# Retention values centred ahead, short pair norms, an output projection begun on half its weight rest, smaller first transfers and a shorter final norm

## The reference, cut to what matters

```python
def retention(q, k, v, g):                      # 6 heads of 64
    ...                                         # rotary, decay-weighted scores sc, causal
    y = (y_intra + y_cross).reshape(b, s, RET_HEADS, HEAD_DIM)
    y = layer_norm(y).reshape(b, s, RET_WIDTH)  # over the 64 columns of a head
    return (jax.nn.silu(g) * y).astype(dt)

def hybrid_layer(x, ...):
    u = rms_norm(x, g_mix_pre) @ w_in
    ...
    mix = jnp.concatenate([y_att, y_conv, y_ret], axis=-1) @ w_out
    x = x + rms_norm(mix, g_mix_post)
    ...
```

## Time and profile before

| | us |
|---|---|
| time, median of 3 runs | 2420.83 |
| profiled execution, its time | 2420.81 |
| its span in the trace | 2419.0 |
| TensorE matmul busy | 2397.8 (99%) |
| VectorE busy | 1587.0 (66%) |
| ScalarE busy | 1084.9 (45%) |
| GpSimd busy | 339.9 (14%) |
| granted TensorE clock, mean | 0.999 of full speed |
| DMA, mean over the span | 108 GB/s |

### The profile page before, as it was taken

How to read it: one execution, slowest core, us unless ns; L and a number is a source line. 1 busy time by engine, 2 the same in 40 slices (tenths; PEclk the granted TensorE clock), 3 DMA queues, 4 the chain that set the end, 5 groups by cost and what they waited for, 6 DMA issues and landing times.

```text
span 2419.0 us, 34256 instructions
## 1 busy us (share of the span) xinstructions
PE 2397.8 (99%) x13622; PEld 2023.0 (84%) x13622; DVE 1587.0 (66%) x2239; ACT 1084.9 (45%) x1615; POOL 339.9 (14%) x259
## 2 busy tenths in 40 slices
PE   9999999999999999999999999999999999999998
PEld 7877988998886889889988888877778788889997
DVE  7764775665976477556643447769995476359685
ACT  4345553544445456345532235522335564325443
POOL 1231020001122102000111123400000121120001
PEclk9999999999999999999999999999999999999999
DMA  4311223323230222232222235643442153222322
GB/s 168 144 44 70 88 87 105 111 83 121 79 137 30 105 71 104 88 122 97 85 100 103 90 109 173 207 173 118 141 142 96 31 179 124 102 99 81 118 88 87
DMA packets 46738, 260.15 MB, mean 108 GB/s; under 512 B 5440, under 2 KB 8000, under 8 KB 22656
## 3 DMA queue, kind: packets, MB, share of 16 engines
q1 hardware_dynamic: 44192, 248.94, 29.3%
q0 software_dynamic: 640, 5.51, 0.6%
q10 hardware_dynamic: 1760, 3.67, 0.5%
HBM read 240.27 MB, written 16.78 MB: 106 GB/s over the span
## 4 chain that ended last, share of the span: by engine, by line
PE 89%; DVE 5%; ACT 2%; issue 2%; DMA 1%; POOL 0%; SPq 0%; DVEq 0%; ACTq 0%
PE gemm L486 58%; PE gemm L1094 5%; PE gemm L1095 5%; PE gemm L1096 5%; DVE w_lo L436 1%; PE gemm L770 1%; PE gemm L781 1%; PE gemm L772 1%; DVE out_sb L1904 1%; ACT w_hi L428 1%; PE turned L1389 1%; PE mixed L1403 1%; PE score L1380 1%; PE gemm L663 1%; PE gemm L664 1%
## 5 line engine op out<-in xcount | busy, mean ns | idle before, releaser
L436 DVE TENSOR_TENSOR w_lo<-w_raw,w_hi 128x2048 fp32r<-128x2048 f32 (+4 forms) x157 | 340.0, 2166 | 199.1 <-ACT w_hi L428 199.0
L486 PE MATMUL gemm<-h_hi,w_hi 128*128 128x512 f32 x1136 | 454.5, 400 | 1.9 <-DVE w_lo L436 1.4
L486 PE MATMUL gemm<-h_hi,w_lo 128*128 128x512 f32 x1136 | 443.3, 390 | 0.0
L486 PE MATMUL gemm<-h_lo,w_hi 128*128 128x512 f32 x1136 | 442.7, 390 | 0.0
L428 ACT ACTIVATE w_hi<-w_raw 128x2048 fp32r<-128x2048 f32 (+4 forms) x167 | 292.9, 1754 | 190.4 <-PE gemm L486 168.5
L486 PEld LDWEIGHTS gemm<-h_hi,w_hi 128*128 128x128 f32 x1136 | 213.7, 188 | 57.4 <-issue 9.1
L486 PEld LDWEIGHTS gemm<-h_hi,w_lo 128*128 128x128 f32 x1136 | 213.2, 188 | 45.8
L486 PEld LDWEIGHTS gemm<-h_lo,w_hi 128*128 128x128 f32 x1136 | 213.7, 188 | 41.8 <-issue 1.0
L486 PE MATMUL gemm<-f_hi,w_hi 128*128 128x512 f32 x480 | 187.2, 390 | 0.6
L486 PE MATMUL gemm<-f_hi,w_lo 128*128 128x512 f32 x480 | 186.8, 389 | 0.0
L486 PE MATMUL gemm<-f_lo,w_hi 128*128 128x512 f32 x480 | 186.8, 389 | 0.0
(11 more groups left out here) (544 smaller groups left out, 5295.9 us busy)
## 6 DMA issues: line engine op xcount, KB each, us to landing
w_raw<-in_w SPq DMA_DIRECT2D x179, 1024.0 KB, 4.8
w_raw<-in_w SPq DMA_DIRECT2D x18, 512.0 KB, 3.8
w_raw<-in_w SPq DMA_DIRECT2D x12, 768.0 KB, 4.2
trig_kept<-made SPq DMA_DIRECT2D x16, 512.0 KB, 5.9
trig<-trig_kept SPq DMA_DIRECT2D x16, 512.0 KB, 6.1
w_raw<-in_w SPq DMA_DIRECT2D x8, 640.0 KB, 4.6
bias_t<-in_att_bias SPq DMA_DIRECT2D x2, 1536.0 KB, 8.9
decay_t<-in_c_decay SPq DMA_DIRECT2D x2, 1536.0 KB, 8.8
```

The costliest lines, as they stand in the source:

```text
L436: dve.tensor_tensor(flat(w_lo, b), flat(w_raw, b), flat(w_hi, b).bitcast(F32), ALU.subtract).then_inc(S["w_rest"], 1)
L486: mm = pe.matmul(dst, lhs, rhs, start=b.first and k == 0 and j == 0, stop=b.last and k == b.kt - 1 and j == 2)
```

## The change

1. **Retention.** The values are centred before they are used: `centre_values` takes the mean over the 64 columns of each head from v, for a pair of heads in one reduction and one fused product on VectorE, at weight block 10 and after steps s = 5 and s = 9. `pair_mean` and `centre` go. ScalarE squares the pair straight from PSUM in `pair_out`. `pair_var` becomes one plain 128x512 matmul with `head_ones`, whose result is already spread, so `pair_spread` goes; Ln and Exp now take 128x512. GpSimd's gate product waits for the copy, no longer for the squares.
2. **Output projection.** `partial` on the first block waits for `half_rest` and, from tile 4 on, for `w_rest`. The second norm steps among the partials go; only `pair_var(3)` stays, after tiles 0 and 1.
3. **Opening.** Block 0 comes as a quarter, a quarter and a half, x tiles 0 and 1 separately; `ones` and `ident` come after all of x and both blocks. ScalarE does all roundings of x before the squares. `keep_clock` runs 4 matmuls, not 6, and the wait for `ones` moves to the sum, which moves two steps later.
4. **Memory sum.** It moves half a tile into the third block of `ffn1_down`.
5. **End.** ScalarE also multiplies x by the final gain (`x2_sq`), 6 tiles during the last blocks, the last two per half. `last_sums` goes: `final_total` takes three plain matmuls per half. `finished` takes one product per group of tiles (two groups of 4; then groups of 3, 3 and 2), with one store per group. The sum of half 0 now stands after the first of the two tiles of half 1, before it stood one step (3 matmuls) ahead of the end of the second.

The diff, cut to its core:

```diff
-            (1, 0), (1, 1), (0, 6), (0, 7), (1, 2), "sum", (1, 3), (1, 4), "turn", (1, 5), (1, 6), (1, 7)]
+            (1, 0), (1, 1), (0, 6), (0, 7), (1, 2), (1, 3), (1, 4), "sum", (1, 5), (1, 6), "turn", (1, 7)]
...
+        CUTS = [(0, WSIZE // 4), (WSIZE // 4, WSIZE // 2), (WSIZE // 2, WSIZE)]
+        FIRST_CUTS, SECOND_CUTS = CUTS, [(0, WSIZE // 2), (WSIZE // 2, WSIZE)]
...
-            load_part(sp, plan[0], False)
-            load_x(0)
-            load_part(sp, plan[0], True)
+            load_part(sp, plan[0], 0)
+            sp.dma_start(x_sb[:, 0, :], x_rows[:, 0, :]).then_inc(x_first_in, 16)
+            sp.dma_start(x_sb[:, 1, :], x_rows[:, 1, :]).then_inc(x_in[0], 16)
+            load_part(sp, plan[0], 1)
+            load_x(2)
+            load_part(sp, plan[0], 2)
+            load_x(4)
+            load_part(sp, plan[1], 0)
+            load_x(6)
+            load_part(sp, plan[1], 1)
             sp.dma_start(ones[:], A["c_ones"]).then_inc(consts_in, 16)
...
-            keep_clock(pe, t_ps[:], rs[:, 0:P], rs[:], 6)
-            pe.wait_ge(consts_in, 32)
+            keep_clock(pe, t_ps[:], rs[:, 0:P], rs[:], 4)
...
             def ret_mixed(s):
+                if j == 0 and h % 2 == 0:
+                    pe.wait_ge(S["v_centred"], cnt("v_centred", h // 2 + 1))
...
             def pair_var(j):
                 pe.wait_ge(S["ln_sq_s"], cnt("ln_sq_s", 2 + j))
-                for q in range(TOKT):
-                    mm = pe.matmul(t_ps[:, 2 * q:2 * q + 2], sq_tile(4 + j)[:, P * q:P * q + P],
-                                   head_ones[:, 0:P:HD], start=True, stop=True)
-                mm.then_inc(S["ln_var"], 1)
+                if j > 1:
+                    pe.wait_ge(S["ln_root"], cnt("ln_root", j))
+                pe.matmul(t_ps[:], head_ones[:], sq_tile(4 + j), start=True, stop=True).then_inc(S["ln_var"], 1)
...
-                if p == 2 and at_step == 0:
-                    pair_spread(1)
                 if p and at_step == TOKT // 2:
-                    pair_mean(p)
-                if p and at_step == TOKT + TOKT // 2:
                     pair_var(p)
...
-            partial(pe, first, h_hi, h_lo, (0, 1), ready=cnt("h_ready", KD))
-            pair_spread(2)
-            partial(pe, first, h_hi, h_lo, (2,), ready=cnt("h_ready", KD))
-            pair_mean(3)
-            partial(pe, first, h_hi, h_lo, (3, 4), ready=cnt("h_ready", KD))
+            partial(pe, first, h_hi, h_lo, (0, 1), ready=cnt("h_ready", KD), front=3 * lay + 1)
             pair_var(3)
-            partial(pe, first, h_hi, h_lo, (5,), ready=cnt("h_ready", KD))
-            partial(pe, second, h_hi, h_lo, (0, 1))
-            pair_spread(3)
-            partial(pe, second, h_hi, h_lo, (2,))
+            partial(pe, first, h_hi, h_lo, (2, 3, 4, 5), ready=cnt("h_ready", KD), front=3 * lay + 1)
+            partial(pe, second, h_hi, h_lo, (0, 1, 2))
...
             def pair_out(p):
                 act.wait_ge(S["ret_mix"], cnt("ret_mix", 2 * TOKT * (p + 1)))
+                act.activation(sq_tile(5 + p), ret_bank[p][:], ACT.Square).then_inc(S["ln_sq_s"], 1)
                 act.activation(out_sb[:, 5 + p, :], ret_bank[p][:], ACT.Copy).then_inc(S["ret_out"], 1)
...
-                layer_norm_sq(1 + p)
                 layer_norm_root(1 + p)
...
+            def centre_values(p):
+                c = ATT_W + P * p
+                pair = values[:, c // WCOLS, :, c % WCOLS:c % WCOLS + P].rearrange("p t (h f) -> p t h f", h=2)
+                total = v_sum[p].rearrange("p (t h) -> p t h", h=2)
+                dve.wait_ge(S["g_free"], plan1[9 if p else 6].t0 + TOKT)
+                step(dve.tensor_reduce(total, pair, AX_X, ALU.add))
+                dve.scalar_tensor_tensor(out=pair, in0=total.unsqueeze(3).broadcast_to([P, TOKT, 2, HD]),
+                                         scalar=-1.0 / HD, in1=pair, op0=ALU.mult,
+                                         op1=ALU.add).then_inc(S["v_centred"], 1)
...
+                to = (o_ps, t_ps)[e][:, 0:HALF]
+                pe.wait_ge(S["sq_added"], FINAL_ADDED)
+                pe.matmul(to, ones[:], out_sb[:, 0, TOKENS[e]], start=True, stop=False)
+                pe.wait_ge(S["squares"], KD * (N0 + 3) + KD - 2 + e + 1)
+                pe.matmul(to, ones[:], out_sb[:, KD - 2, TOKENS[e]], start=False, stop=False)
+                pe.matmul(to, ones[:], out_sb[:, KD - 1, TOKENS[e]], start=False, stop=True).then_inc(S["norm_sum"], 1)
...
-                        if (e, m, k) == (1, 1, b.kt - 2):
+                        if (e, m, k) == (1, 0, b.kt - 1):
                             final_total(0)
...
+                root = rs[:, TOKENS[e]].unsqueeze(1).broadcast_to([P, k1 - k0, HALF])
+                dve.tensor_tensor(out_sb[:, k0:k1, TOKENS[e]], x2_sq[:, k0:k1, TOKENS[e]], root,
+                                  ALU.mult).then_inc(S["final_s"], 1)
```

More of the change, by code:

```diff
@@ L499, in tile_in, with partial @@
             return a[k] if isinstance(a, list) else a[:, k, :]
-        def partial(pe, b, hi, lo, ks, ready=None):
+        def partial(pe, b, hi, lo, ks, ready=None, front=None):
             if ks[0] == 0:
-                pe.wait_ge(S["w_rest"], b.n + 1)
+                if front is not None:
+                    pe.wait_ge(S["half_rest"], front)
+                else:
+                    pe.wait_ge(S["w_rest"], b.n + 1)
             wh, wl = view(w_hi, b), view(w_lo, b)
             for k in ks:
+                if front is not None and k == KD // 2:
+                    pe.wait_ge(S["w_rest"], b.n + 1)
                 if ready is not None:
@@ L1327, in begin_vector @@
             dve.wait_ge(first_par_in, 16)
-            rest_part(dve, plan[0], False)
+            rest_part(dve, plan[0], 0)
             for k in range(KD):
                 raw_rest(dve, 0, k, gain)
-                if k == 0:
-                    rest_part(dve, plan[0], True)
+                if k == 1:
+                    rest_part(dve, plan[0], 1)
+                if k == 3:
+                    rest_part(dve, plan[0], 2)
                 if k == 5:
[L1334 to L1338, removed]
+                    rest_part(dve, plan[1], 0)
+            for k in range(1, 4):
+                add_square(dve, 1, k, out_sb)
+            rest_part(dve, plan[1], 1)
+            for k in range(4, KD):
                 add_square(dve, 1, k, out_sb)
@@ L2045, in layer_vector @@
             rest_mixed(5)
-            centre(3)
             rest_mixed(6)
@@ L2692, in third_tensor @@
                                 tile_ready=None if j else (S["g2_s"], F2T + sum(GATED_PARTS[:part])))
+            FINAL_ADDED = added_by(5) - 1
             def final_total(e):
-                pe.wait_ge(S["sq_added"], last_added(e) + 2)
-                pe.matmul((o_ps, t_ps)[e][:, 0:HALF], ones[:], out_sb[:, 0, TOKENS[e]], start=True,
-                          stop=True).then_inc(S["norm_sum"], 1)
+                to = (o_ps, t_ps)[e][:, 0:HALF]
[4 more added lines that the diff above has]
+                pe.matmul(to, ones[:], out_sb[:, KD - 1, TOKENS[e]], start=False, stop=True).then_inc(S["norm_sum"], 1)
             pe.wait_ge(S["w_rest"], b.n + 1)
@@ L3773, in last_half, with finished @@
                                          op1=ALU.add).then_inc(S["g_free"], 1)
-            def last_sums(e):
-                dve.wait_ge(S["squares"], KD * (N0 + 3) + KD - 2 + e + 1)
-                dve.wait_ge(S["sq_added"], last_added(0))
-                one, two, total = [out_sb[:, k, TOKENS[e]] for k in (KD - 2, KD - 1, 0)]
-                dve.tensor_tensor(one, one, two, ALU.add).then_inc(S["sq_added"], 1)
-                dve.wait_ge(S["sq_added"], last_added(e) + 1)
-                dve.tensor_tensor(total, total, one, ALU.add).then_inc(S["sq_added"], 1)
-            def finished(e, tiles):
+            def finished(e, part):
+                k0, k1 = FINAL_TILES[e][part]
                 dve.wait_ge(S["rs_ready"], N0 + 4 + e)
-                for k in tiles:
-                    dve.scalar_tensor_tensor(out=out_sb[:, k, TOKENS[e]], in0=x_sb[:, k, TOKENS[e]],
-                                             scalar=gains2["final"][:, k:k + 1], in1=rs[:, TOKENS[e]], op0=ALU.mult,
-                                             op1=ALU.mult).then_inc(S["final_s"], 1)
+                root = rs[:, TOKENS[e]].unsqueeze(1).broadcast_to([P, k1 - k0, HALF])
+                dve.tensor_tensor(out_sb[:, k0:k1, TOKENS[e]], x2_sq[:, k0:k1, TOKENS[e]], root,
+                                  ALU.mult).then_inc(S["final_s"], 1)
             last_half(0)
-            last_sums(0)
+            finished(0, 0)
             last_half(1)
-            finished(0, range(3))
-            last_sums(1)
-            finished(0, range(3, KD))
-            finished(1, range(KD))
+            finished(0, 1)
+            for part in range(3):
+                finished(1, part)
         with nc.Block() as block:
```

165 lines of the change are left out of this document (84 added, 81 removed).

## The result

The changed kernel takes 2407.49 us (median of 5 runs, 2407.07 to 2408.05), where the kernel before took 2420.82 beside it: ratio 0.9945, interval 0.9931 to 0.996. The forecast was 2407.2. The profiled execution, which was the slowest of the five, has a span of 2406.2 us for 2419.0: 12.8 us less, where the medians differ by 13.3.

The account below looks back on a forecast made before the run. TensorE, busy 99% of the span, bounds the kernel: only time off its queue or the two ends counts. Opening −2.5, retention −10.0, memory sum −0.3, end −0.8 sum to −13.6: 2407.2 us, range 2403.5 to 2412.5.

Parts of the forecast that it names:

- the opening: Start of the kernel: four clock-keeping matmuls end at 7.3 us, next product starts at 30.5 against 32.98, −2.5 us.
- the part in front of the projection: Retention, each layer: the output projection starts at 197.9 instead of 200.47, −2.6 us.
- the part behind it: After the projection's start, each layer: −4.2 us of removed norm steps, +1.6 for variance and a wait, −2.6 us.
- all before 7.3: Opening: quarter block and x tile 0 land about 4.6 and 5.5 us, rounding ends about 6.2, before `keep_clock` ends.
- Rival D: Opening: smaller transfers bring nothing, opening −1.2, the rest as forecast, 2408.5 us; chance 0.78 together with the main forecast.
- so `ret_mixed(17)` on PE ends at 194.1: Retention, step 17 on TensorE: this product ends at 194.1 us instead of 194.48, though PE is ready 1.1 us earlier.
- mixed 0.58 + 0.36: Retention, last mixed products on TensorE before the projection: they take 0.58 + 0.36 us, ending at 197.9.
- new stall: Output projection, ahead of `pair_var(3)`: TensorE waits 0.7 us for ScalarE's square of pair 3, done at 201.4.
- GpSimd starts its gate product earlier; nobody waits: Retention: GpSimd's gate product starts earlier and no engine waits for it; no time was charged.
- A: Retention: nothing waits, so −6.4 us per layer, 2404.4 us; chance 0.08.
- B: Retention: ScalarE holds the projection's start at the old 200.5, only the part behind is gained: −8.8, 2412.0 us; chance 0.10.
- C: Opening: PE drops to 1.2 GHz, its 23.2 us of work take up to 46.4, 2430.4 us; chance 0.04.

Follow-up runs that it names:

- the kernel with the variance late: Changed kernel with third pair's centring after step 7, VectorE's rests of tiles 0 and 1 after step 17, and pair 3's variance after tile 2: 2407.64 us.
- the moves of VectorE's steps: Changed kernel with third pair's centring after step 7 and VectorE's rests of tiles 0 and 1 after step 17: third block to projection 165.93 us.

## Why the prediction was right

The sum held (13.6 forecast, 12.8 on the span, 13.3 on the medians), and its largest term, 10.0 for retention, was measured at 10.0. Term by term it was less good than its sum: the opening was 0.6 too good, the part in front of the projection 1.0 too good per layer and the part behind it 0.8 too bad, so part of the closeness is luck.

**Opening, 2.5 forecast, 1.9 measured.** In the profiled execution the mechanism was the one forecast: `keep_clock` set the start and no later step stalled. One size was off. Six of its eight records and part of the seventh ran at 0.85 us, where I had taken 5.4 from the kernel before (there it was four and part of the fifth; my sum counted the tail of the last record as well). The last record started at 7.43 and held PE for 0.43 more, to 7.86 for 7.3; that is why the first real matmul, which the trace puts at 7.46, takes 0.64 us to the next. From 7.86 to 31.05 is 23.2 us, as forecast.

That size is not a property of the kernel. With the same four `keep_clock` matmuls, from three to six full records ran at 0.85 us in the ten kernels, and in five of them the row was over before the data was there. Then TensorE waited for ScalarE's rounding of x tile 0, as in the kernel with the variance late:

```profile
1.53 5.21 PE L1248 MATMUL turned<-rs 128*128 128x512 f32 x8 [1.53 <-DVE rs L1359]
7.54 0.47 PE L673 MATMUL gemm<-h_hi,w_hi 128*128 128x512 f32 x1 [0.79 <-ACT h_hi L617]
```

So the data and the clock-keeping row end at about the same time, and "all before 7.3" was wrong about the data: both inputs of the first matmul are ready between 7.0 and 7.5 us. I let the small transfers come at the old byte rate (4.6 us). The rate itself was lower, 0.24 MB by 3.9 us for 0.36 with the first two transfers merged, and the first weights were usable at 5.8. The rule of the Trainium skill that speaks against small transfers (DMA: Bandwidth & Descriptors, Measured), and which stands there for transfers issued from GpSimd, has this much right; yet merging them cost 0.73, so the trace decides for the small ones. Rival D, which gave them nothing, falls.

**Retention, 5.2 per layer worked out, 5.0 taken, 4.94 and 5.06 measured.** The total was right through two errors that cancel. In front of the projection I forecast 2.6 and got 1.57; behind it 2.6, and got 3.37. The steps that failed:
- "so `ret_mixed(17)` on PE ends at 194.1". Read on the time axis of the changed kernel that is 192.2; it ended at 192.78. I gave the second product of a pair half of the pair's time, some 0.5 us after its input. The products of two heads write different halves of the partitions and run side by side, 0.91 us for both, when both inputs are there. One that ends by itself takes about as long: started at 191.77, it let the next instruction begin at 192.78. So the pair costs 1.0 us from its second input, whichever way the first goes, and the 0.60 us by which VectorE makes the second later than the first is not hidden.
- "mixed 0.58 + 0.36". The four last products took 1.29 us for 0.94, and had taken 199.55 − 198.36 = 1.19 in the kernel before, so this was misread. The last pair needs 0.56, as before, since its two inputs come 0.2 us apart.
- the **new stall** of 0.7 in front of `pair_var(3)`. ScalarE's square ended at 199.32, on my estimate of its queue (199.5 on that axis), but TensorE came at 199.86, 1.2 later than I had it, mostly by the two slips above, and too late to wait. One term was 1.0 too good, the other 0.8 too bad.
- "GpSimd starts its gate product earlier; nobody waits". It is true that nobody waits for it, but it slows the VectorE instruction beside it by 0.8 us. In the changed kernel that was nearly covered (TensorE reaches step 22 0.1 us later); it took away what the moves of VectorE's steps were to bring.

The forecast that VectorE's centring is covered by the wait on step 16 was right (the kernel with the centring after step 7: 165.93 and 165.92). `half_rest` is worth 0.8 per layer, as forecast (0.8 between 197.9 and 198.7).

**Memory sum, 0.3 forecast:** 1443.40 − 1442.21 = 1.19 became 1432.47 − 1431.57 = 0.90: right.

**End, 0.8 forecast, 0.5 measured.** VectorE ended 1.0 us earlier, measured from the start of the last block (forecast 1.1). The stores took the rest back: from VectorE's end to the end of the span 3.06 us, before 2.58. The forecast had them nearly right, 1 MB at 0.38 MB/us as the last limit: on the axis of the kernel before, the last store landed at 2418.1, for 2418.0. But its own figures, 2418.0 for 2418.7, give 0.7 and not the 0.8 that went into the sum, and the last landing before was at 2418.6.

**Rivals.** A (nothing waits) gave 6.4 per layer, 1.4 more than was found. B (ScalarE holds the start at the old time) falls: the start moved. C, the slow side, falls: half speed ended within the clock-keeping row in all ten kernels, and even without any such matmuls it lasted for 5.0 us of work and the third block came 1.9 us later, not 20.

## What to carry to other kernels

Work out what an engine's queue loses, then ask of each engine beside it what it now does at the same time: a product on GpSimd that nobody waits for can hold up VectorE's step beside it for 0.8 us. When several waits lie on top of each other, taking away one or two gains nothing, so read the next trace for the wait that has come up before trusting the step. And check the parts of a sum against marks in the trace, since a total within 0.1% can hide two terms that are each off by 1 us.

## What the runs showed of the hardware that I had not expected

- Two plain matmuls of 512 columns into different halves of the partitions overlap almost wholly: 0.91 us for the pair, where one that ends by itself takes about 1.0. They overlap too when the second starts late, but then the pair lasts until 1.0 us after that start, 1.60 us in all.
- A VectorE difference of 128x1024 takes 1.21 us alone and 1.64 to 2.18 us when it starts inside a GpSimd product of 1.27 us; it then ends 1.08 us after that product in all seven kernels where this was read. Started first, it holds the product up instead, 1.93 us for 1.27. So which of the two is delayed is decided by which starts first. A product of VectorE with one input in PSUM was not delayed.
- TensorE's first phase at half speed differs from one execution to the next although the work is the same: it lasted from 3.1 to 6.0 us after the first of the eight clock-keeping records, 4.2 us in the kernel before and 5.0 us in the kernel without them. The granted clock in the profile shows 1.00 throughout, so the phase must be read from the starts (0.85 us for a record that later takes 0.43).
